# Row scaling of the second and third attention moved to GpSimd, with the late bias tables between its steps and a lag of four steps

## The reference, cut to what matters

```
B: 8 heads of 64, chunk-causal over 512 tokens
   p = softmax(q k^T * scale + rel_table[head, clipped distance]);  o_b = p v
C: 4 heads of 128, over 256 memory rows
   p = softmax(q mk^T * scale);  o_c = p mv
```

## Time and profile before

| | us |
|---|---|
| median of three runs (2282.06, 2284.85, 2284.83) | 2284.83 |
| the profiled execution | 2282.84 |
| its span | 2280.3 |
| PE busy in the span | 2238.8 (98%) |
| DVE, ACT, POOL busy | 1179.0, 964.5, 229.5 |

### The profile page before, as it was taken

One profiled execution on the slowest core, in us unless ns is written; L12 is line 12 of the kernel. 1 busy time (PEld: TensorE's weight loads), 2 busy tenths in 40 slices (PEclk: granted clock), 3 DMA queues, 4 the chain that ended last, 5 costly groups with the idle time before them and its releaser, 6 DMA issues.

```text
span 2280.3 us, 29997 instructions
## 1 busy us (share of the span) xinstructions
PE 2238.8 (98%) x11038; PEld 1797.9 (79%) x11038; DVE 1179.0 (52%) x2092; ACT 964.5 (42%) x1582; POOL 229.5 (10%) x247
## 2 busy tenths in 40 slices
PE   8999999999999999999999999999999999999998
PEld 6888888877868888888888887787566788888887
DVE  7434436675475556434435656754666554432432
ACT  7332223456585333332223422634788434322322
POOL 2000001100210001000001420000443001000011
PEclk9999999999999999999999999999999999999999
DMA  6322322311302232322332382232000132332331
GB/s 244 111 87 86 113 94 80 111 56 56 111 11 92 83 110 95 109 92 83 104 108 69 103 255 72 68 96 74 2 2 34 60 111 93 110 92 92 96 107 55
DMA packets 213646, 206.81 MB, mean 91 GB/s; under 512 B 4880, under 2 KB 194576, under 8 KB 213296
## 3 DMA queue, kind: packets, MB, share of 16 engines
q1 hardware_dynamic: 210544, 192.31, 26.8%
q0 software_dynamic: 3008, 13.24, 1.8%
HBM read 199.25 MB, written 4.19 MB: 89 GB/s over the span
## 4 chain that ended last, share of the span: by engine, by line
PE 90%; DVE 5%; ACT 2%; issue 2%; DMA 1%; POOL 0%; SPq 0%; ACTq 0%; DVEq 0%; POOLq 0%
PE ps L906 26%; PE ps L908 26%; PE ps L907 26%; PE ps L705 3%; PE ps L732 2%; PE ps L1138 2%; DMA wraw<-in_w_in 1%; DVE Sm L855 1%; PE ps L1047 1%; PE ps L1178 1%; DVE wlo L571 1%; PE ps L1203 1%; ACT whi L564 0%; ACT Sm L803 0%; PE ps L1157 0%
## 5 line engine op out<-in xcount | busy, mean ns | idle before, releaser
L906 PE MATMUL ps<-hH,whi 128*128 128x512 f32 x1528 | 601.1, 393 | 2.2 <-DVE wlo L571 2.2
L908 PE MATMUL ps<-hH,wlo 128*128 128x512 f32 x1528 | 594.7, 389 | 0.0
L907 PE MATMUL ps<-hL,whi 128*128 128x512 f32 x1528 | 594.6, 389 | 0.0
L571 DVE TENSOR_TENSOR wlo<-wraw,whi 128x2048 fp32r<-128x2048 f32 x192 | 441.3, 2299 | 285.8 <-ACT whi L564 285.8
L564 ACT ACTIVATE whi<-wraw 128x2048 fp32r<-128x2048 f32 x192 | 367.0, 1911 | 504.5 <-PE ps L908 494.9
L906 PEld LDWEIGHTS ps<-hH,whi 128*128 128x128 f32 x1528 | 286.3, 187 | 66.1 <-issue 3.3
L907 PEld LDWEIGHTS ps<-hL,whi 128*128 128x128 f32 x1528 | 286.3, 187 | 62.5 <-issue 3.1
L908 PEld LDWEIGHTS ps<-hH,wlo 128*128 128x128 f32 x1528 | 286.3, 187 | 60.4
L906 PE MATMUL ps<-gH,whi 128*128 128x512 f32 x608 | 237.2, 390 | 0.0
L908 PE MATMUL ps<-gH,wlo 128*128 128x512 f32 x608 | 236.6, 389 | 0.0
L907 PE MATMUL ps<-gL,whi 128*128 128x512 f32 x608 | 236.6, 389 | 0.0
(11 more groups left out here) (376 smaller groups left out, 2674.1 us busy)
## 6 DMA issues: line engine op xcount, KB each, us to landing
wraw<-in_w_in SPq DMA_DIRECT2D x45, 1024.0 KB, 5.1
wraw<-in_ffn_wg SPq DMA_DIRECT2D x22, 1024.0 KB, 5.2
wraw<-in_ffn_wu SPq DMA_DIRECT2D x22, 1024.0 KB, 5.1
wraw<-in_w_up SPq DMA_DIRECT2D x16, 1024.0 KB, 5.2
wraw<-in_w_down SPq DMA_DIRECT2D x16, 1024.0 KB, 5.7
wraw<-in_ffn_wd SPq DMA_DIRECT2D x16, 768.0 KB, 4.6
wraw<-in_w_gate SPq DMA_DIRECT2D x12, 1024.0 KB, 4.9
wraw<-in_ffn_wd SPq DMA_DIRECT2D x16, 640.0 KB, 4.3
```

The source lines that it names most:

```text
L571: dve.tensor_tensor(wlo[s][:, :], wraw[s][:, :], f32(whi[s][:, :]), ALU.subtract).then_inc(w_lo[s], 1)
L906: pe.matmul(o, lh, rh, start=start, stop=False)
L907: pe.matmul(o, lh, rl, start=False, stop=False)
L908: return pe.matmul(o, ll, rh, start=False, stop=stop)
```

## The change

B and C get a lag of four, in the general PE order (the order of N is now chosen by name, not by lag). Their multiplication by the reciprocal sum moves from DVE to POOL, which goes through all 48 steps; four of the table steps (`bias_of(6)` to `bias_of(9)`, that is tables 4 to 7, and the loads of raw blocks 6 and 7) stand behind POOL's steps 7, 9, 15 and 17. With a ring of five and a lag of four, DVE has a new wait before it overwrites a row buffer: the transposes of five steps earlier. The counters of N go on from 48.

```diff
@@ lag_of @@
-            return 6 if kind == "A" else 4 if kind in "NX" else 3
+            return 6 if kind == "A" else 4
@@ Step @@
-                self.Sm = ring[k % len(ring)]
+                self.Sm, self.rows = ring[k % len(ring)], len(ring)
@@ steps @@
-            by_pool = 0
+            by_pool = 48 if names[0] == "N0" else 0
             for e in seq:
-                on_pool = e.kind == "N" and e.m != "c"
+                on_pool = e.kind in "BCN" and e.m != "c"
@@ pool_attention @@
-        def pool_attention(pool, names):
-
-            for e in steps(names)[0]:
+        def pool_attention(pool, names, behind={}):
+
+            for k, e in enumerate(steps(names)[0]):
                 if not e.p:
                     continue
                 pool.wait_ge(s_recip, e.p)
-                pool.tensor_scalar(e.Sm[:, 0:e.n], e.Sm[:, 0:e.n], st[:, 16 + e.s % 8:17 + e.s % 8], gate_of(e),
-                                   ALU.mult, ALU.mult).then_inc(s_pool, 1)
+                r_ = st[:, 16 + e.s % 8:17 + e.s % 8]
+                if e.kind == "N":
+                    pool.tensor_scalar(e.Sm[:, 0:e.n], e.Sm[:, 0:e.n], r_, gate_of(e), ALU.mult, ALU.mult).then_inc(s_pool, 1)
+                else:
+                    pool.tensor_scalar(e.Sm[:, 0:e.n], e.Sm[:, 0:e.n], r_, None, ALU.mult).then_inc(s_pool, 1)
+                if k in behind:
+                    behind[k]()
@@ pe_attention @@
-            if lag == 4:
-                for slot in range(0, len(seq) + 4, 2):
+            if names[0] == "N0":
+                for slot in range(0, len(seq) + lag, 2):
                     scores_from(slot)
-                    turns_from(slot - 4)
-                    values_from(slot - 6, 2)
+                    turns_from(slot - lag)
+                    values_from(slot - lag - 2, 2)
@@ dve_attention @@
                     dve.wait_ge(s_full, e.s + 1)
+                    if e.kind in "BC" and slot >= e.rows:
+
+                        dve.wait_ge(t_full, seq[slot - e.rows].u + 1)
@@ gpsimd @@
-            for h in range(8 + 2):
+            def bias_of(h):
+
...
+            for h in range(6):
+                bias_of(h)
+            pool_attention(pool, ["B", "C"], {7: lambda: bias_of(6), 9: lambda: bias_of(7), 15: lambda: bias_of(8), 17: lambda: bias_of(9)})
```

## The result

The changed kernel is slower. Its median is 2288.92 us over 16 runs (2285.48 to 2291.21), that of the kernel before, timed beside it, 2282.46 over 16 (2279.36 to 2284.85). The ratio is 1.0027, 95% interval 1.0019 to 1.0034, so some 6.2 us more, where 2279.3 and 4.4 us less were forecast. It lies outside the range of 2276.3 to 2284.

What follows compares the result with a forecast made beforehand. PE was taken as the bound, broken in B where tables stretch DVE's multiply. Terms -3.7 - 0.4 - 2.3 + 1.5 + 0.5 = -4.4 us, off the 2283.65 average, gave 2279.3; range 2276.3 to 2284, leaving out 2 in 10.

Steps and rivals of the forecast that it cites:

- Part 7: B and C: POOL's multiply (0.77 us) and DVE's pass (0.67) at 512 columns don't stretch each other; nothing.
- part 4: B: late tables on POOL's queue delay its multiplies, PE waits 0.6 to 0.7 us per table; +1.5 us.
- part 6: B and C: DVE's mask-and-maximum waits for earlier transposes, but the chain of some 3.0 us plus 0.6 fits; nothing.
- DVE's multiply and the tables: B and C: moving DVE's multiply away ends PE's idle times where tables stretch it; -3.7 us.
- The merged phases: B: two steps' transposes join in one PE phase, saving 0.16 us for each of fifteen pairs; -2.3 us.
- ACT sets the pace: Rival, B: ACT holds eight steps to 8.88 us, total 2282.0; chance 0.22, shared with costlier tables.
- The tables in POOL's way: B: late tables on POOL's queue hold up multiplies PE's transposes wait for; +1.5 us, ends 0 and 6.9.
- The start: Start of B: POOL's hand-over lengthens the first chains while ACT evicts the held tile; +0.5 us.
- the drain: Last steps of C: one step more of lag leaves PE more work during the last chain; -0.4 us.
- DVE's new wait: B and C, odd steps: mask-and-maximum held at most 0.6 us behind the scores; nothing, at most 2.4 us.
- The slow rival: B: tables fully uncovered (6.9 us) and PE's clock falls (5.1), 2289.2 us; chance 0.07, with costlier starts and hand-overs.
- signs of being wrong the first: B: the forecast is wrong if PE still waits 1 us or more at one step.

Runs made afterwards that it cites:

- e2: Changed kernel, POOL's multiply in B and C given a second multiply by immediate 1.0; ratio 0.9983, last transposes ahead of B to gates (B with C) 59.14 us.
- e8: Kernel before without tables 4 to 7 and their raw loads (heads 4 to 7 use tables 0 to 3); ratio 0.9994, B with C 59.67 us.
- e5: e2 without tables 4 to 7 and their raw loads (heads 4 to 7 use tables 0 to 3); ratio 0.9988, B with C 59.12 us.
- e3: Changed kernel with the multiply back on VectorE and tables off GpSimd's step list, lag of four kept; ratio 1.0002, B with C 61.81 us.
- e9: e2 without the row sums of ScalarE's exponents in B and C (stale factors); one run, B with C 58.20 us.
- e12: The kernel of e2 unchanged, run again in more rounds; ratio 0.9983, B with C 59.17 us.
- e4: Kernel before with N's GpSimd multiply in the form with one operation, gate factor left out; one run, 2292.65 us.
- e1: Changed kernel, GpSimd's multiply in B and C given a second multiply by a column of ones; ratio 0.9985, B with C 59.49 us.
- e10: Changed kernel, GpSimd's multiply in B and C given a second operation adding 0.0; one run, B with C 59.17 us.

## Why the prediction was wrong

The step that failed is the duration of GpSimd's multiply. Part 7 ("POOL against DVE") put it at nothing, and the walk of part 4 and the chain of part 6 gave B's multiply N's 0.45 to 0.77 us, though the diff shows another form for B and C: N's row is of two operations on two columns, the new line has one operation. The prediction doesn't mention the difference. Measured, the new line takes 0.59, 0.92, 1.24 and 1.56 for 128 to 512 columns. The prediction kept no upper end for it, against the plain fact that no row of the trace showed this form. The nearest other row of POOL on 512 columns, the table's 1.27, would have been one.

What it costs: 67.21 - 59.14 = 8.1 us in B with C, from the kernel after to e2. (The ratios of the launches, 1.0027 and 0.9983, say some 10, with 2 us to either side of each.) The other terms of the sum can be read on the fast form:

- *DVE's multiply and the tables* (-3.7): -3.09, by e8. The mechanism held, the size was somewhat high: without the late tables the first twelve steps still take 13.18 in e8, where my count of the losses came to 12.8, and the pass from 637.40 to 646.64 still takes 9.24.
- *The merged phases* (-2.3): nothing in the steady passes (9.24 merged in e5, 9.24 and 9.16 unmerged in e8). PE is busy for 8.91 in a merged pass and for 9.20 and 9.11 in an unmerged one, so merging saves 0.05 to 0.07 per pair and not 0.16, and PE then waits 0.32 for ScalarE's copy. The rival "ACT sets the pace" was right on this.
- *The tables in POOL's way* (+1.5): nothing over the whole of B with C (59.12 in e5, 59.14 in e2). The delay itself comes: the first twelve steps take 12.88 in e2 and 12.35 in e5, 0.5 where my walk had 1.4. I missed that the next pass gives it back (8.74 against 9.24).
- *The start* (+0.5), *the drain* (-0.4) and *DVE's new wait* (0): no run takes them apart. e5 and e8 differ by lag, order and host of the multiply, and by 59.67 - 59.12 = 0.55 us in all. The parts of it (0.8 less in the first twelve steps, 0.4 more from the last pass's end to the gates) belong in part together, since with the longer lag a step's transposes move from the one into the other. DVE's new wait costs nothing that shows: e3, which has it and leaves the multiply on DVE, takes 9.23 in its last pass, where e8, without it, takes 9.16 and 9.24.

So the merged phases, the start, the drain and the new wait bring 0.55 us together, where the sum had 2.2. That -4.4 was near what the fast form gives (-3.6 in B with C, ratio 0.9983, some -3.9) is luck: the errors of these terms stood against each other. And the one duration without a row turned the sign.

The slow rival had 2289.2, and 2288.92 was measured, but that is a coincidence: the granted clock stayed at 1.00 in all windows of B and C, and POOL sat on the path through its own multiplies. Of the prediction's signs of being wrong the first didn't show either: PE never waited 1 us at one step. It waited 12 times, at most 0.73 each, 6.8 us in all.

The Trainium skill has a rule that bears on this. GPSIMD Engine Reference, Elementwise — side-by-side cycle accounting, says that up to two operations an element costs 1.03 cycles, limited by the ports. With the clock of 1.2 GHz that the same page gives under Specifications, that is by estimate 0.86 ns an element. e2 agrees: from 0.478 at 256 to 0.692 at 512 columns is 0.84 ns. The form with one operation does not: 0.923 to 1.560 is 2.49 ns, three times that. The measurement decides. By that rule the new line would have cost what e2's costs, and the change would have come out near my forecast.

What stays open: B with C accounts for 4.45 us of the 6.2. In the two profiles the stretch from N's first scores to the first copy of the final output is 1.4 us longer after than before (621.6 against 620.2), with the same instructions. Most of that is TensorE's clock at N's start. It fell to 0.50 in both, but counted from N's first scores later in the kernel after (the first 4 us have 0.83 before and 1.00 after), and came back later. A phase of values in the kernel before, then a window of 4 us at the same place of N, before and after:

```profile
1594.93 2.57 PE L1157 MATMUL ps<-PTc,vcp 128*64 128x512 f32 x8
1595.40:1599.40 4.00, 4.00 (x19) 1.31 (x16) 1.01 (x7) 1.78 (x9) 1.26 (x3) 0.89 0.00 0
1599.90:1603.90 4.00, 4.00 (x14) 0.97 (x10) 0.44 (x3) 0.94 (x5) 0.83 (x2) 0.62 0.01 2
```

PE is busy throughout both windows, and the granted clock is 0.89 before and 0.62 after. The phase of values that took 2.57 us before took 3.64 after (at 1599.49), 1.07 more. Whether the change brings that, or the two executions differ by chance, is not shown: e9, with the fast form, has the same long stretch (621.7), and e2 and e12, which are one kernel, differ by 0.4 (620.9 and 620.5). But the clock does go with the time from run to run. Of the 16 runs of the kernel after, six had a mean granted clock of 0.992 and took 2289.5 to 2291.2 us, and the one with 0.995 took 2285.5. It was not tried either how the tables could be made cheaper than their 1.27 us.

## What to carry to other kernels

A duration belongs to a form, that is operation, operand kinds and their number, not to an instruction's name: when work is moved to an engine, find a row of exactly that form or keep a bound above it, and add up the busy time of the new host against the pass (here 8.6 us of multiplies and 2.5 of two tables in a pass of 9.2, which can't fit). When an engine is relieved of a wait, name what sets the pace next, and let a delay count only if that one has no slack to give it back. Two halves that look independent (a deeper lag, a move to a slower engine) may each be worth little and more together, here 0.9 and 0.9 against 3.6 us.

## What the runs showed of the hardware

- GpSimd's `tensor_scalar` in float32 in place takes 0.59, 0.92, 1.24 and 1.56 us for 128, 256, 384 and 512 columns with one operation by a column (the kernel after, and e4 in N); with a second one by an immediate 0.37, 0.48, 0.58 and 0.69 (e2), by a column 0.45, 0.56, 0.67 and 0.77 (e1). A second operation that changes nothing, a multiply by 1.0 (e2) or an added 0.0 (e10), more than halves the instruction at 512.
- VectorE's multiply of 512 columns takes 0.49 alone and 1.53 to 1.84 beside GpSimd's sum of two tensors. With the late tables gone, its longest in the whole launch was 0.489 (e8). VectorE's pass with one input from PSUM keeps its 0.69 for 512 columns beside GpSimd's multiply of either form (the kernel after, e2).
